# TensorE passes eleven of the meetings between stages without waiting, in a 27-stage transformer program on one core

## What is computed

```python
# second block, layer = 0, 1; h is (256, 1024)
h = h + 0.5 * swiglu(rmsnorm(h, g1), wg1, wu1, wd1)            # RowFfn up1/down1
h = h + mixer(rmsnorm(h, gm), ...)                             # layer 0: "even", layer 1: "odd": Project, Attention, Residual
q = rmsnorm(h, mg) @ wq                                        # Project wq: 1 job of 512 columns
k, v = split(rmsnorm(mem, sg) @ wkv)                           # Project wkv: its rows are the memory, not h
h = h + softmax(norm(q) @ norm(k).T * scale) @ v @ wo          # Attention, Residual wo
h = h + 0.5 * swiglu(rmsnorm(h, g2), wg2, wu2, wd2)            # RowFfn up2/down2
```

## Time and profile before

| | |
|---|---|
| median of 3 runs | 1686.58 us (1685.48 to 1687.38) |
| profiled execution, its own time | 1686.16 us |
| its span | 1684.4 us |
| TensorE busy | 1630.6 us, 97% |
| VectorE, ScalarE, GpSimd busy | 1026.1, 863.7, 23.9 us |
| mean granted TensorE clock | 0.99 |

### The profile page before, as it was taken

One profiled execution on the slowest core, in us unless ns is written; L12 is line 12 of the kernel. 1 busy time (PEld: TensorE's weight loads), 2 busy tenths in 40 slices (PEclk: granted clock), 3 DMA queues, 4 the chain that ended last, 5 costly groups with the idle time before them and its releaser, 6 DMA issues.

```text
span 1684.4 us, 20987 instructions
## 1 busy us (share of the span) xinstructions
PE 1630.6 (97%) x8509; PEld 1378.3 (82%) x8509; DVE 1026.1 (61%) x1392; ACT 863.7 (51%) x1194; POOL 23.9 (1%) x27
## 2 busy tenths in 40 slices
PE   9989998999999999999999999999999999999999
PEld 8877877999888888877777888888888878788887
DVE  5565667698755554567856555455554775765553
ACT  5355564576545443554655544354434564654442
POOL 0000002000000000000000000000000000000000
PEclk9988999999999999999999999999999999999999
DMA  7733334765554555444143655545554533434553
GB/s 285 282 144 125 109 117 152 285 230 177 189 186 167 183 180 195 177 152 147 35 166 110 239 179 195 182 180 189 178 197 175 183 118 106 169 125 175 188 187 125
DMA packets 42960, 289.96 MB, mean 172 GB/s; under 512 B 5048, under 2 KB 5198, under 8 KB 9968
## 3 DMA queue, kind: packets, MB, share of 16 engines
q1 hardware_dynamic: 38272, 271.93, 44.9%
q0 software_dynamic: 4592, 16.69, 2.9%
HBM read 287.51 MB, written 8.55 MB: 176 GB/s over the span
## 4 chain that ended last, share of the span: by engine, by line
PE 86%; DVE 7%; ACT 3%; DMA 2%; issue 1%; DVEq 0%; PEldq 0%; SPq 0%; POOL 0%; PEld 0%; ACTq 0%
PE bank L481 25%; PE bank L483 25%; PE bank L482 25%; PE bank L487 6%; DVE low L447 2%; PE bank L763 2%; DMA raw<-stream_dram 2%; ACT high L436 1%; PE bank L1386 1%; PE bank L1697 1%; PE bank L645 1%; DMA h<-x_dram 0%; PE bank L1909 0%; DVEq L2631 0%; DVE stat L681 0%
## 5 line engine op out<-in xcount | busy, mean ns | idle before, releaser
L447 DVE TENSOR_TENSOR low<-raw,high 128x2048 fp32r<-128x2048 f32 x254 | 581.1, 2297 | 381.9 <-ACT high L436 381.4
L436 ACT ACTIVATE high<-raw 128x2048 fp32r<-128x2048 f32 x256 | 486.8, 1913 | 355.9 <-DMA raw<-stream_dram 348.2
L481 PE MATMUL bank<-high,xh 128*128 128x512 f32 (+1 forms) x1232 | 486.5, 395 | 5.5 <-DVEq L2631 4.2
L483 PE MATMUL bank<-high,xl 128*128 128x512 f32 (+1 forms) x1232 | 478.4, 388 | 0.0
L482 PE MATMUL bank<-low,xh 128*128 128x512 f32 (+1 forms) x1232 | 477.4, 388 | 0.0
L481 PEld LDWEIGHTS bank<-high,xh 128*128 128x128 f32 x1232 | 232.4, 189 | 53.1 <-issue 3.9
L483 PEld LDWEIGHTS bank<-high,xl 128*128 128x128 f32 x1232 | 231.9, 188 | 48.0
L482 PEld LDWEIGHTS bank<-low,xh 128*128 128x128 f32 x1232 | 232.6, 189 | 44.3
L481 PE MATMUL bank<-high,hh 128*128 128x512 f32 x440 | 172.0, 391 | 0.0
L483 PE MATMUL bank<-high,hl 128*128 128x512 f32 x440 | 171.5, 390 | 0.0
L482 PE MATMUL bank<-low,hh 128*128 128x512 f32 x440 | 171.4, 390 | 0.0
(11 more groups left out here) (239 smaller groups left out, 1553.2 us busy)
## 6 DMA issues: line engine op xcount, KB each, us to landing
raw<-stream_dram SPq DMA_DIRECT2D x257, 1024.0 KB, 4.8
band_wide_dram<-band_rows_dram POOLq DMA_DIRECT2D x1, 3072.0 KB, 33.7
t_wide_dram<-t_rows_dram POOLq DMA_DIRECT2D x1, 2304.0 KB, 16.9
u<-mem_dram POOLq DMA_DIRECT2D x2, 1024.0 KB, 5.2
bias<-band_wide_dram POOLq DMA_DIRECT2D x1, 2048.0 KB, 12.2
rel_wide_dram<-rel_rows_dram POOLq DMA_DIRECT2D x1, 1920.0 KB, 18.4
bias<-t_wide_dram POOLq DMA_DIRECT2D x1, 1536.0 KB, 10.6
bias<-rel_wide_dram POOLq DMA_DIRECT2D x1, 1280.0 KB, 7.1
```

What stands on the lines that cost most here:

```text
L436: act.activation(self.high[:, n % RING, :], self.raw[:, n % RING, :], ACT.Copy).then_inc(self.high_split, 1)
L447: dve.tensor_tensor(self.low[:, n % RING, :], self.raw[:, n % RING, :], self.high[:, n % RING, :].bitcast(F32), ALU.subtract).then_inc(sel ...
L481: pe.matmul(out, lh, rh, start=start, stop=False)
L483: return pe.matmul(out, ll, rh, start=False, stop=stop)
```

## The change

Three parts, and nothing moves on ScalarE, VectorE and SyncE.

1. In front of eleven stages TensorE still drains and counts itself in `stage_done`, but no longer waits for the others. It waits instead for `cleared`, which GpSimd raises behind each clearing of semaphores, to a value of one stage earlier. The eleven are the seven stages behind a residual sum without gain (10, 13, 17, 18, 19, 22, 26), the two whose rows are the memory (14, 23), and the even and the odd attention (11, 20). For the attentions the projection's `tensor` gets waits at its end (`leads`).
2. In the seven stages tiles 0 to 3 are multiplied first. Tiles 4 and 5 are transposed behind k = 0, tiles 6 and 7 behind k = 1, the first pair once `sum_added` says that all quarters are in `h`.
3. `rows_added` and `next_low`, which were cleared each stage, become `sum_added` and `early_low`, which count through the program.

```diff
+    def after(self, pe, s, k):
+        if self.early and 2 * k < KT - self.early:
+            if k == 0:
+                pe.wait_ge(self.core.sum_added, self.sums_needed)
+            self.tensor(pe, s, self.early + 2 * k, self.early + 2 * k + 2)
+
     def next(self, pe, s, k):
+        if self.early:
+            return
         self.tensor(pe, s, k + self.early + self.AHEAD, k + self.early + self.AHEAD + 1)

     def arrive(self, pe, s, k):
+        if self.early and k == 0:
+            pe.wait_ge(self.core.early_low, self.early_needed)
...
     def tensor(self, pe, s):
-        if self.source:
+        if self.source and not self.source.early:
             self.source.tensor(pe, s)
...
+                if self.source and n == 0:
+                    self.source.after(pe, s, k)
...
+        if self.leads:
+            self.rows_there(pe, s, len(self.jobs) - 2)
+            pe.wait_ge(s["turned_by_act"], self.turn.drained("act", len(self.turn.by) - 1))
+            if self.shared:
+                pe.wait_ge(s["turned_by_dve"], self.turn.drained("dve", len(self.turn.by) - 1))
+            if self.select:
+                pe.wait_ge(s["keys_positive"], len(self.select.UNITS))
...
                 core.release(last, self.up, i)
+                if c == 0:
+                    self.rows.after(pe, s, k)
...
-            stage.following.begin_early()
+            stage.following.begin_early(early, stage.sums_before + len(stage.order))
+            early += stage.following.early
+            then.ahead = True
+        if isinstance(then, Project) and then.source and then.source.rows is not c.h:
+            then.ahead = True
+        if isinstance(stage, Project) and isinstance(then, Attention) and len(stage.jobs) > 2:
+            stage.leads = then.ahead = True
...
-    def meet(engine, n):
+    def meet(engine, n, wait=True):
         engine.drain().then_inc(core.stage_done, 1)
+        if not wait:
+            return
         engine.wait_ge(core.stage_done, 4 * (n + 1))
         engine.nop(nofuse=True)
...
+                if stage.ahead:
+                    pe.wait_ge(core.cleared, n - 1)
                 stage.tensor(pe, core.sets[n % 2])
-                meet(pe, n)
+                meet(pe, n, wait=n + 1 == len(stages) or not stages[n + 1].ahead)
...
                     pool.sem_clear(range(other[0], other[-1] + 1))
+                    pool.drain().then_inc(core.cleared, 1)
```

More of the change, by code:

```diff
@@ L312 @@
          "norm_means", "norm_roots", "inverse_ready", "wide_ready", "wide_turned", "row_ready", "scaled_ready",
-         "quarter_done", "rows_added", "next_turned", "next_high", "next_low", "fill_summed", "fill_stored",
+         "quarter_done", "next_turned", "next_high", "fill_summed", "fill_stored",
          "branch_filled", "heads_joined", "products_ready", "branch_added",
@@ L393, in __init__ @@
         self.high_split, self.low_split, self.slot_used = sem("high_split"), sem("low_split"), sem("slot_used")
+        self.sum_added, self.early_low, self.cleared = sem("sum_added"), sem("early_low"), sem("cleared")
         self.stage_done, self.loaded, self.stored = sem("stage_done"), sem("loaded"), sem("stored")
@@ L497 @@
 class Stage:
+    ahead = False
     def __init__(self, core):
@@ L745, in __init__ @@
         self.early = 0
+        self.sums_needed = None
         self.step = 2 if base == 0 and tiles == KT and gain is None else 1
@@ L748, in __init__, with begin_early @@
         self.gain = PARAM(core.param, "gains")[:, n:n + KT] if gain else None
-    def begin_early(self):
+    def begin_early(self, early_before, sums_needed):
         self.early, self.banks = 4, tuple(range(8))
+        self.early_needed, self.sums_needed = early_before + self.early, sums_needed
     def bank(self, k):
@@ L791, in early_lows @@
             dve.wait_ge(s["next_high"], k + 1)
-            self.low(dve, k).then_inc(s["next_low"], 1)
+            self.low(dve, k).then_inc(self.core.early_low, 1)
     def tensor(self, pe, s, first=0, end=KT):
@@ L955, in __init__ @@
         self.select = select
+        self.leads = False
         self.masked = masked
@@ L1088, in gpsimd @@
                 cut, _ = self.quarter(b, half)
-                pool.wait_ge(s["rows_added"], n + 1)
+                pool.wait_ge(c.sum_added, self.sums_before + n + 1)
                 pool.dma_start(self.store[:, b, cut], c.h[:, b, cut]).then_inc(c.stored, 16)
@@ L1119, in tensor @@
             if n == 2 and self.following:
-                pe.wait_ge(s["rows_added"], 2)
+                pe.wait_ge(c.sum_added, self.sums_before + 2)
                 self.following.early_tensor(pe, s)
@@ L1169, in vector @@
             dve.scalar_tensor_tensor(c.h[:, b, cut], ps, self.row_factor(b), c.h[:, b, cut], ALU.mult, ALU.add)\
-               .then_inc(s["rows_added"], 1)
+               .then_inc(c.sum_added, 1)
     def add_normed(self, dve, s, last):
@@ L2614, in stages_of @@
                       store=out.rearrange("a (b p) d -> p (a b) d", p=P) if layer else None))
+    sums = early = 0
+    for stage in st:
+        if isinstance(stage, Residual) and stage.gain is None:
+            stage.sums_before = sums
+            sums += len(stage.order)
     for stage, then in zip(st, st[1:]):
```

## The result

| | before | change |
|---|---|---|
| median of 9 runs each | 1686.62 us (1685.43 to 1690.40) | 1699.74 us (1683.29 to 1712.00) |
| ratio, with its 95% interval | | 1.0055 (1.0032 to 1.0078) |
| profiled execution, its own time | 1686.16 us | 1712.00 us |
| mean granted TensorE clock in it | 0.990 | 0.973 |
| TensorE busy | 1630.6 us | 1660.1 us |

The change is slower: by 13 us in the medians, by 5 to 13 us (the interval of the ratio) in the means. The ratio is one of means and leaves out the slow execution of 1712.00 us. The forecast was 1684.5 (1675.5 to 1688.5), "within 0.2%" at 0.60; it did not hold. The nine times of the change lie 29 us apart, those of before 5, and they go with the mean granted clock: 0.993 in the fastest execution (1683.29), 0.982 in the median one, 0.973 in the slowest, which is the profiled one.

The account below looks back on a forecast made before the run. TensorE was taken as the bound, busy 1630.6 of 1684.4 us, its idle time mostly the meeting of all engines. Terms +1.0 - 0.7 + 2.3 - 3.9 - 0.8 = -2.1 us on the median 1686.58 gave 1684.5, range 1675.5 to 1688.5.

Parts of the forecast that it names:

- within 0.2%: Whole kernel: time no further from before than a measurement tells, about 0.2% or 3.4 us; chance 0.60.
- the even attention: At the even attention's start: TensorE scores and fills early at full clock, first turn 793.5 instead of 797.23; -3.9 us.
- the clock falls in the even attention: Rival: the new wait there lowers the clock, first turns and scores at half speed, 1.5 to 3 us; about 1686.8; chance 0.15.
- Restart 0.20: At stages where TensorE no longer waits for the meeting: drain and restart still cost 0.20 us.
- Wait for the split at k = 4, 0.8: Four wide stages and both query projections: TensorE waits 0.8 us at the fifth k for VectorE's split of slot 2.
- Wide seams +0.22 to +0.28: Both second feed-forwards, layer-1 first one, odd projection: slot 2 starts 0.22 (two seams) or 0.28 (two) later, +1.0 together.
- T: Modelled end of a stage's last matmul; at wide seams TensorE was to go on at T + 7.56.
- Even projection -0.7: Seam from residual sum to even projection: no stall for the split, so the removed wait saves 0.7 us.
- Query and memory rows +1.06 and +1.26: Query projection to memory rows: late splits delay VectorE's output copy, +1.06 and (layer 1) +1.26; +2.3 together, query seams included.
- Odd projection and attention, +0.2 and -0.8: Odd projection, one of four wide seams: 0.22 or 0.28 later; odd attention: idle 0.98 becomes restart 0.20, -0.8.
- The idle time simply goes: Rival, all eleven seams: slot 2 and the output copy are not late, -10.8 us, 1675.8; chance 0.18.
- The restart is dear: Rival, head of each changed stage: restart costs 0.95, as much as the meeting; +3.9 us, 1690.5; chance 0.07.

Follow-up runs that it names:

- x11: The change with 36 instead of 16 filler matmuls before the even attention and 10 at the start of stage 12: 1687.84 us, ratio 1.0009.
- x3: The kernel before, with TensorE passing its meeting without waiting at the even attention alone, 16 fillers: 1694.55 us, ratio 1.0069.
- x8: x3 with 36 fillers in place of 16 in front of the even attention: 1684.10 us, ratio 0.9989.
- x6: x5 with ten filler matmuls added at the start of stage 12, the even output stage: 1681.21 us, ratio 0.9974.
- x1: The change, but TensorE waits at the meeting in front of the even attention again: 1687.51 us, ratio 1.0011.
- x2: The change with 36 filler matmuls in place of 16 in front of the even attention: 1687.57 us, ratio 1.0000.
- x4: x2 with VectorE's split of slot 2 put ahead of the low parts of tiles 4 to 7: 1686.69 us, ratio 0.9998.
- x5: x2 with all four late tiles transposed behind k = 0, none behind k = 1: 1684.51 us, ratio 0.9995.
- x7: The change at the seven residual seams only; memory rows and both attentions wait at the meeting as before: 1694.42 us, ratio 1.0052.
- x9: x6 with VectorE taking one split less ahead of its copy of the query's output: 1678.48 us, ratio 0.9949.
- x12: The change with the even attention's 16 fillers behind the first turn of probabilities instead of ahead of the pause: 1700.92 us, ratio 1.006.
- x13: x12 with 32 fillers behind the first turn instead of 16: 1694.06 us, ratio 1.0051.

## Why the prediction was wrong

**The failed step** is the even attention: the sum took it at -3.9 with the clock at 1.00, and the rival "the clock falls in the even attention" had a chance of 0.15 and, above all, a price of "1.5 to 3 us". Both profiles of the change have the fall, and their stretch over the even projection and attention is 20.4 us over before, where the sum had -4.6. The rival named the right place, the right wait ("from 791.1 to 793.5"; it was 790.95 to 793.30) and the right effect ("first turns and scores run at half speed"). The price was taken from one pair of rows, in which a low clock lasted 5.55 us and ended by itself. Those rows held the answer to another question: how long the clock stays low when 28 matmuls in one piece follow the pause. The change moves just those ahead of the pause. In the profiled execution of the change the fall lasted 61 us and cost 186.56 - 161.63 = 24.9 us of the stretch against x11's; in x3 the two falls cost 14.6. No execution near the median of the change (1699.74, clock 0.982) was profiled; since the one at 0.993 took 1683.29, its falls were probably of a middle length. With that price even the rival's upper end, 1687.5, lay inside the range, which ended at 1688.5.

**The other steps**, by the change without falls (x11) unless another is named:

- *Restart 0.20*: 0.26 at all seven residual seams of the change (0.36 at one of x11), 0.10 in front of the attention and 0.11 in front of the memory rows. The Trainium skill, "TensorE: Matmul & The Clock Gate", step-by-step part, says that weight loads are pulled ahead of running matmuls; the prediction reckoned 0.03 if that held past a drain. The rows speak against it here: in the change the load of the seam's first matmul starts at 1132.52, 0.03 ahead of its matmul and not during the one before. Whether the drain or the waits behind it hold the load back, no run shows., 0.23, was the better guide.
- *Wait for the split at k = 4, 0.8*: 0.77 to 0.80 at the four wide stages and both query projections, none at the even projection. Right.
- *Wide seams +0.22 to +0.28*: the three feed-forward stretches are +0.45, +0.39 and +0.50. Right in kind, mis-sized by about 0.2 each: TensorE goes on at T + 7.70 and not 7.56, since it starts 0.15 behind VectorE's end (1139.84 to 1139.99), not 0.03. The first matmul behind that wait is followed by the next after 0.31 instead of 0.227, which the forecast counted at three other places and not at this one.
- *Even projection -0.7, even attention -3.9*: x8 has -3.94 for the attention alone, x11 -4.56 for both, so -0.6 for the projection. Right.
- *Query and memory rows +1.06 and +1.26*: stretches 12-16 and 21-25 are +1.05 and +1.40. The sum is right, in part by luck: in the change's profile the query seam takes 0.51 of it (forecast 0.28), and the memory's first matmul stands 3.56 behind T and not 3.8. In that profile the second stretch is +2.85: behind a pause of 1.91 us its clock fell as well (granted clock 0.75 in the window 1466:1469).
- *Odd projection and attention, +0.2 and -0.8*: stretch 18-21 is -0.41. Right within 0.2.
- Sum -2.1: -1.2, by one execution of each kernel.

**The other rivals.** "The idle time simply goes" (1675.8) is excluded by the waits at k = 4. "The restart is dear" needed 0.88 and had 0.26. The order of tiles, which the forecast took as given, is worth 1.0 us at each wide seam and 6.2 us over all stretches (x6 against x11; some 5 were expected), more than the removed waits.

**Open.** When the clock falls. Between 817 and 836 us, around the end of the even attention, it fell in the profiles of x1 to x5, x7, x9 and x12, and not in those of before, x6, x8, x11 and x13. The short waits there do not tell the two apart: they are 0.74, 0.92, 0.72 and 1.48 us in x5, with a fall, and 0.74, 0.92, 0.72 and 1.64 in x8, without. Open with it are why the fall behind the pause lasts 20 us in one execution and 61 in another, and why x11's median lies 6 us over its profiled execution.

## What to carry to other kernels

Before you take out a wait, look at what stands behind it, not only at how long it is: filler matmuls placed behind a wait do their work there, and once they are moved ahead of the wait that is left, a pause of 2.35 us can cost, as in the two profiled executions of the change, ten times its own length. Read the granted clock beside the busy share, since an engine at half clock shows as fully busy. When one in-order engine is let ahead, write down what the next one does in its own order: here turning four tiles at once instead of two and two, and one copy ahead of one split, were worth more than the eleven waits (6.2 and 2.5 us against 1.2, by the stretches).

## What the runs showed of the hardware

- A pause of 2.35 us (790.95 to 793.30) in front of small matmuls was followed by granted clock 0.50 from about 795 to 856 us in the change, through the rest of the attention and into the next stage, and for 20 us in x3. From 800 to 810 us TensorE was shown busy 10.00 of 10.00 us with 32 matmuls. At 1.2 GHz four score matmuls of 256 columns took 2.07 us instead of 1.13.
- After a pause of 4.46 us, 16 matmuls of 256 columns (3.76 us) did not bring the clock back in the profiled execution of x12; of the 32 in x13, the last ran at 1.00.
- Where TensorE drained and the waits behind were already met, 0.26 us passed to the next stage's first matmul of a weight slot, and 0.10 to 0.11 us to scores or transposes.
- From the end of VectorE's split to the matmul that waited for it, 0.15 us passed (1139.84 to 1139.99).
